# Output stage of the first recurrent scan made inside the scan: bonuses during the rounds, norms and gates between the last chain's steps

## What is computed

```python
g = jax.nn.sigmoid(xg) @ g_up
for direction in range(2):
    a = jax.nn.sigmoid(a_gate0[direction] + xa @ a_gate_up[direction])
    ys.append(wkv7_scan(hs(r), hs(decay), hs(k_dir), hs(v), kk, hs(a), reverse=(direction == 1)))
    a_dirs.append(a)
y = ys[0] + ys[1]
mean = jnp.mean(y, axis=-1, keepdims=True)
var = jnp.mean(jnp.square(y - mean), axis=-1, keepdims=True)
yn = ((y - mean) * lax.rsqrt(var + LNX_EPS)).reshape(B, S, RWKV_WIDTH) * lnx_g + lnx_b
k_bonus = hs(k * (1.0 + (0.5 * (a_dirs[0] + a_dirs[1]) - 1.0) * k_a))
bonus = jnp.sum(hs(r) * k_bonus * r_k, axis=-1, keepdims=True) * hs(v)
return (yn + bonus.reshape(B, S, RWKV_WIDTH)) * g
```

## Time and profile before

| | us |
|---|---|
| median of 3 runs | 2873.18 (2870.74 to 2874.13) |
| the profiled execution's own time | 2872.07 |
| its span | 2869.4 |
| the last full round of the scan (n = 7) | 590.0 to 620.6 |
| the last chain, its products and sum | 620.6 to 637.2 |
| output stage, to the first instruction of the next stage | 637.2 to 667.3 |

### The profile page before, as it was taken

One profiled execution on the slowest core, in us unless ns is written; L12 is line 12 of the kernel. 1 busy time (PEld: TensorE's weight loads), 2 busy tenths in 40 slices (PEclk: granted clock), 3 DMA queues, 4 the chain that ended last, 5 costly groups with the idle time before them and its releaser, 6 DMA issues. The chain is left out here.

```text
span 2869.4 us, 45446 instructions
## 1 busy us (share of the span) xinstructions
PE 2383.1 (83%) x17090; PEld 1374.9 (48%) x17090; DVE 1587.3 (55%) x3634; ACT 1000.6 (35%) x2575; POOL 962.6 (34%) x765
## 2 busy tenths in 40 slices
PE   6998979988898777777777777777779989889996
PEld 3544679975664222332223222332248878643333
DVE  6665465644566666767676666766554453430002
ACT  2122633333433333333333333333245232433433
POOL 0000021113136555555555545545530143223331
PEclk9999989999999999999999999999999966889998
DMA  9942100003069999999999999999963220369994
GB/s 373 374 168 85 56 13 4 5 30 123 32 260 420 420 421 418 417 417 415 413 415 413 413 415 413 415 411 413 415 238 104 98 58 2 123 259 356 378 356 175
DMA packets 174634, 770.12 MB, mean 268 GB/s; under 512 B 33728, under 2 KB 51792, under 8 KB 95056
## 3 DMA queue, kind: packets, MB, share of 16 engines
q0 software_dynamic: 87552, 545.34, 46.5%
q1 hardware_dynamic: 68176, 183.94, 17.3%
q10 hardware_dynamic: 18688, 37.95, 3.7%
HBM read 815.37 MB, written 16.78 MB: 290 GB/s over the span
## 5 line engine op out<-in xcount | busy, mean ns | idle before, releaser
L2108 PE MATMUL bank<-weight_slots,diagonals 128*128 128x512 f32 x1024 | 485.2, 617 | 160.5 <-ACT diagonals L2051 160.5
L1990 DVE SCALAR_TENSOR_TENSOR weight_slots<-weight_slots,h_rows 128x1024 f32<-128x1024 f32 x320 | 392.1, 1225 | 247.8 <-DMA weight_slots<-in_uv,expert_idx 247.0
L1758 POOL DMA_INDIRECT weight_slots<-in_uv,expert_idx x320 | 405.5, 1267 | 353.1 <-PE bank L2108 273.1
L2108 PE MATMUL bank<-expert_rows,first_scores 128*128 128x512 f32 x768 | 370.5, 619 | 147.4 <-ACT first_scores L2051 143.5
L2108 PEld LDWEIGHTS bank<-weight_slots,diagonals 128*128 128x128 f32 x1024 | 188.2, 194 | 449.4 <-ACT diagonals L2051 260.0
L1758 POOL DMA_INDIRECT expert_rows<-in_uv,expert_idx x192 | 283.6, 1477 | 314.2 <-PE bank L2108 185.3
L2040 ACT ACTIVATE expert_act<-expert_dot 128x2 f32<-128x2 f32 x256 | 52.0, 203 | 846.6 <-DVE weight_slots L1990 613.2
L1990 DVE SCALAR_TENSOR_TENSOR expert_rows<-expert_rows,h_rows 128x1024 f32<-128x1024 f32 x192 | 235.3, 1226 | 154.0 <-DMA expert_rows<-in_uv,expert_idx 153.8
L2108 PEld LDWEIGHTS bank<-expert_rows,first_scores 128*128 128x128 f32 x768 | 137.9, 192 | 371.8 <-ACT first_scores L2051 236.7
L682 PE MATMUL bank<-rhs_hi,w_lo 128*128 128x512 f32 (+1 forms) x440 | 178.1, 405 | 33.2 <-POOL rhs_lo L638 18.0
L602 DVE TENSOR_TENSOR w_lo<-weight_slots,w_hi 128x384 fp32r<-128x384 f32 (+3 forms) x152 | 102.7, 682 | 168.7 <-ACT w_hi L547 168.3
(11 more groups left out here) (531 smaller groups left out, 4094.7 us busy)
## 6 DMA issues: line engine op xcount, KB each, us to landing
expert_w<-in_experts SPq DMA_DIRECT2D x55, 1024.0 KB, 12.1
expert_w_more<-in_experts SPq DMA_DIRECT2D x41, 1024.0 KB
mod_w<-in_ada_w ACTq DMA_DIRECT2D x17, 2048.0 KB, 11.8
mod_w<-in_ada_w SPq DMA_DIRECT2D x7, 2048.0 KB, 16.1
weight_slots<-in_w_in SPq DMA_DIRECT2D x6, 2048.0 KB, 17.7
weight_slots<-in_w_in SPq DMA_DIRECT2D x8, 1536.0 KB, 6.7
att_bias<-in_att_bias SPq DMA_DIRECT2D x8, 1024.0 KB, 6.9
weight_slots<-in_w_out SPq DMA_DIRECT2D x4, 2048.0 KB, 8.8
```

Of the source, the lines that this page charges most:

```text
L1758: pool.indirect_dma_start(self.rows[n % self.SLOTS], None, self.core.dram["uv"], bass.IndirectOffsetOnAxis(self.idx[:, t, column:column + ...
L1990: dve.scalar_tensor_tensor(out=u, in0=u, scalar=1.0, in1=hN[:, t, :], op0=ALU.mult, op1=ALU.mult, accum_out=dot[:, j:j + 1]).then_inc(dott ...
L2108: mm = pe.matmul(bank[2 * (t % 2) + half][:, :], diag[j], rows[j][:, D + half * S:D + half * S + S], start=column == 0, stop=column == HK - 1)
```

## The change

`stage_rwkv_output` is removed, and its steps are put into the scan's programs. The bonus of pair f is made by POOL and ACT in the rounds: POOL adds the two rates behind `reads(2f + 1)`, ACT scales the sum behind level 3 of round 2f (`scale_bonus`), and POOL multiplies twice more. The gate's sigmoid is made as exp on ACT in round 3, and 1 + x and a reciprocal on DVE at the end of round 4 (`squash_gate`). In the last chain PE makes a list `SIDE` of 14 matmuls of 128x512, one behind each half-step, with `y_of_chunk` behind each second one, and ACT moves their results. The inverse root is now Sqrt on ACT and a reciprocal on DVE (`invert`), three of which stand between the half-steps of the last chain and the fourth behind it. The third multiply of the bonus goes from DVE to POOL, and the gate is copied out of PSUM by ACT. Results lie in tiles that the scan no longer reads (`a`, `sig`, `kk`). The scan's tiles are placed anew so that the three lent slots are free once the last `end_products` is made, and their loads are issued there; `g_up` is loaded in the rounds.

The diff, cut to its core:

```diff
@@ stage_rwkv
         stage_rwkv_scan(core, zr, sig, a, kk, sel, restart, mixed)
-        stage_rwkv_output(core, zr, a, sel, mixed)
@@ stage_rwkv_scan: placement, order
-        place = [work[:, i, :] for i in range(21)] + [lent[:, i, :] for i in range(8 * RING)]
...
+        ahat, y0, u_sb, states, gain = own[14:19]
+        m_rb, m_rk = [lent[0], own[19]], [lent[1], own[20]]
+        e1, e2, inv, invT, ka, xs = lent[2:8]
...
+        bonus, rstd, gate = [[of[:, f, :] for f in range(PAIRS)] for of in (a, sig, kk)]
+        SIDE = (("centre", 0), ("centre", 1), ("bonus", 0), ("bonus", 1), ("centre", 2), ("sum", 0), ("sum", 1), ("bonus", 2), ("sum", 2),
+                ("gate", 0), ("bonus", 3), ("gate", 1), ("gate", 2), ("gate", 3))
@@ sync
+                sp.wait_ge(summed, 7 + 4)
+                sp.dma_start(g_up, core.dram["g_up"]).then_inc(g_loaded, 16)
+                sp.wait_ge(end_full, 3 * ROUNDS)
+                core.ring.load(sp, core.ring.issued + RING)
@@ vector
+                def squash_gate():
+                    dve.wait_ge(gate_raised, 1)
+                    dve.tensor_scalar(gate_in, gate_in, 1.0, None, ALU.add).then_inc(gate_plus, 1)
+                    dve.wait_ge(gate_plus, 1)
+                    dve.reciprocal(gate_in, gate_in).then_inc(gate_squashed, 1)
+                def invert(f):
+                    dve.wait_ge(rooted, f + 1)
+                    dve.reciprocal(rstd[f], rstd[f]).then_inc(inverted, 1)
...
+                        if n == 0 and l == 1:
+                            columns_of_output()
                     add_y(n - 1)
                     gains(n)
+                    if n == 4:
+                        squash_gate()
+                last = PAIRS - 1
                 for hs in range(14):
                     chain(ROUNDS - 1, hs)
+                    if hs in (8, 9, 11):
+                        invert((8, 9, 11).index(hs))
+                    if hs in (10, 12, 13):
+                        norm((10, 12, 13).index(hs))
                 add_y(ROUNDS - 1)
+                for f in range(last):
+                    add_bonus(f)
+                for f in range(last):
+                    store(f)
+                invert(last)
+                norm(last)
+                add_bonus(last)
+                store(last)
@@ gpsimd
+                def bonus_of(f):
+                    pool.wait_ge(summed, 7 * (2 * f + 1) + 6)
+                    pool.tensor_tensor(bonus[f], a[:, f, :], a[:, f + 4, :], ALU.add).then_inc(rated, 1)
+                    pool.wait_ge(bonus_scaled, f + 1)
+                    pool.tensor_tensor(bonus[f], bonus[f], zr[:, K + f, :], ALU.mult).then_inc(keyed, 1)
+                    pool.wait_ge(keyed, f + 1)
+                    pool.tensor_tensor(bonus[f], bonus[f], zr[:, R + f, :], ALU.mult).then_inc(weighed, 1)
                 for n in range(1, ROUNDS):
                     rates(n)
                     reads(n)
+                    if rev_of(n):
+                        bonus_of(pair_of(n))
+                for f in range(PAIRS):
+                    pool.wait_ge(b_copied, f + 1)
+                    pool.tensor_tensor(bonus[f], bonus[f], zr[:, V + f, :], ALU.mult).then_inc(bonused, 1)
@@ scalar
+                def scale_bonus(f):
+                    if f == 0:
+                        act.wait_ge(cols_made, 2)
+                    act.wait_ge(rated, f + 1)
+                    act.activation(bonus[f], bonus[f], ACT.Identity, scale=cols[:, f, 0:1], bias=cols[:, f, 1:2]).then_inc(bonus_scaled, 1)
...
+                        if l == 3 and not rev_of(n):
+                            scale_bonus(pair_of(n))
+                        if l == 3 and n == 3:
+                            act.wait_ge(summed, 7 * 3 + 4)
+                            act.activation(gate_in, zr[:, 13, :], ACT.Exp, scale=-1.0).then_inc(gate_raised, 1)
...
+                act.activation(core.root[:, 0:1], core.ones[:, 0:1], ACT.Sqrt)
+                for what, f in SIDE:
...
+                square(PAIRS - 1)
+                take_root(PAIRS - 1, S3_BANK)
@@ tensor
                 for hs in range(14):
-                    chain(ROUNDS - 1, hs)
-                y_products(ROUNDS - 1, range(NC))
+                    chain(n, hs)
+                    if hs % 2 == 0:
...
+                        y_of_chunk(n, hs // 2)
+                    side(hs)
+                pe.wait_ge(u_out, 7 * n + 7)
+                y_of_chunk(n, NC - 1).then_inc(y_full, 1)
+                pe.wait_ge(y_added, PAIRS)
+                pe.matmul(C_BANK[last][:, :], centre[:, :], mixed[:, 4 + last, :], start=True, stop=True).then_inc(y_centred, 1)
+                sum_squares(last, S3_BANK)
```

More of the change, by code:

```diff
@@ L1154, in stage_rwkv_scan @@
         z_bank, w_bank = bank[0:2], bank[2:4]
+        C_BANK, S3_BANK = (bank[2], bank[3], bank[1], bank[4]), bank[5]
+        SIDE = (("centre", 0), ("centre", 1), ("bonus", 0), ("bonus", 1), ("centre", 2), ("sum", 0), ("sum", 1), ("bonus", 2), ("sum", 2),
+                ("gate", 0), ("bonus", 3), ("gate", 1), ("gate", 2), ("gate", 3))
+        TURNS = [step for step in SIDE if step[0] != "centre"]
+        side_bank = lambda step: bank[0] if TURNS.index(step) % 2 == 0 else bank[7]
         def columns(ap, m, half):
@@ L1353, in copy_y, with square, take_root @@
                         act.activation(mixed[:, 4 + pair_of(n), :], Y_BANK[:, :], ACT.Copy).then_inc(y_copied, 1)
+                def scale_bonus(f):
[3 more added lines that the diff above has]
+                    act.activation(bonus[f], bonus[f], ACT.Identity, scale=cols[:, f, 0:1], bias=cols[:, f, 1:2]).then_inc(bonus_scaled, 1)
+                def square(f):
+                    act.wait_ge(y_centred, f + 1)
+                    act.activation(rstd[f], C_BANK[f][:, :], ACT.Square).then_inc(squared, 1)
+                def take_root(f, ps):
+                    act.wait_ge(sq_summed, f + 1)
+                    act.activation(rstd[f], ps[:, :], ACT.Sqrt, scale=1.0 / HD, bias=64e-5).then_inc(rooted, 1)
                 decays(0, 0)
@@ L1380, in _ @@
                         act.activation(to, bank[END_BANK[j]][:, :], ACT.Copy).then_inc(end_out, 1)
-                copy_y(ROUNDS - 1)
+                act.activation(core.root[:, 0:1], core.ones[:, 0:1], ACT.Sqrt)
+                for what, f in SIDE:
+                    if what == "centre":
+                        square(f)
+                    elif what == "sum":
+                        take_root(f, side_bank((what, f)))
+                    elif what == "bonus":
+                        act.wait_ge(b_summed, f + 1)
+                        act.activation(bonus[f], side_bank((what, f))[:, :], ACT.Copy).then_inc(b_copied, 1)
+                    else:
+                        act.wait_ge(g_full, f + 1)
+                        act.activation(gate[f], side_bank((what, f))[:, :], ACT.Copy).then_inc(g_copied, 1)
+                square(PAIRS - 1)
+                take_root(PAIRS - 1, S3_BANK)
             @block.tensor
@@ L1490, in chain, with y_of_chunk @@
                         mm.then_inc(u_full, 1)
+                def y_of_chunk(n, k):
+                    c = order(n)[k]
+                    for h in range(2):
+                        pe.matmul(chunk(Y_BANK, c, h), chunk(u_sb if k else y0, c, h), chunk(m_rb[n % 2], c, h), start=True, stop=False)
+                    for h in range(2):
+                        mm = pe.matmul(chunk(Y_BANK, c, h), chunk(vN[n % 2], c, h), chunk(m_rk[n % 2], c, h), start=False, stop=k == 0)
+                    if k >= 1:
+                        for h in range(2):
+                            mm = pe.matmul(chunk(Y_BANK, c, h), chunk(states, k, h), chunk(rho[n % 2], c, h), start=False, stop=True)
+                    return mm
                 def y_products(n, ks):
@@ L1499, in y_products @@
                     for k in ks:
-                        c = order(n)[k]
-                        for h in range(2):
-                            pe.matmul(chunk(Y_BANK, c, h), chunk(u_sb if k else y0, c, h), chunk(m_rb[n % 2], c, h), start=True, stop=False)
-                        for h in range(2):
-                            mm = pe.matmul(chunk(Y_BANK, c, h), chunk(vN[n % 2], c, h), chunk(m_rk[n % 2], c, h), start=False, stop=k == 0)
-                        if k >= 1:
-                            for h in range(2):
-                                mm = pe.matmul(chunk(Y_BANK, c, h), chunk(states, k, h), chunk(rho[n % 2], c, h), start=False, stop=True)
+                        mm = y_of_chunk(n, k)
                     if NC - 1 in ks:
@@ new lines, in sum_squares, with side @@
+                def sum_squares(f, ps):
+                    pe.wait_ge(squared, f + 1)
+                    pe.matmul(ps[:, :], core.headones[:, :], rstd[f], start=True, stop=True).then_inc(sq_summed, 1)
+                def side(i):
+                    what, f = SIDE[i]
+                    if what == "centre":
+                        if f == 0:
```

(21 more changed lines are left out.)

164 lines of the change are left out of this document (38 added, 126 removed).

## The result

| | before | after |
|---|---|---|
| median of 20 runs | 2871.53 us (2867.69 to 2876.40) | 2878.31 us (2874.68 to 2883.06) |
| profiled execution: own time, span | 2872.07, 2869.4 | 2881.73, 2879.9 |

A forecast was written before the change was run, and what follows sets the result against it. PE's queue was taken to bound the rounds, with hand-overs in the last chain and output stage; 9.6 + 3.1 + 8 - 9.9 = +10.8 us on 2872.07 gave 2882.9, so 2884 as median, range 2875 to 2891.

The forecast's parts named there:

- ACT's wait in rounds 2, 4 and 6: Behind level 3, ACT waits for POOL's sum before evacuating level 4, delaying PE's end products: 3.2 us each, 9.6 us.
- The reciprocal at the end of round 4: 1 + x and a 3.33 us reciprocal on DVE precede the chain's first half-step; PE goes on 3.1 us later.
- The clock: Each of four stalls idles PE over 3 us and lowers its clock: 2 us each, 8 us in all.
- round 0: First round of the scan: POOL's sum is early and ACT's 0.8 us lie before level 4, so no cost.
- The tail: From the last chain to the end of the last store: ends 9.9 us earlier, 11.6 at full clock throughout.
- Its first step: Last chain's half-step pairs: a 128x512 matmul holds PE 0.86 us, a pair takes 2.3, half-step 8 starts at 629.8.
- the basis: Forecast's starting time: one execution's own time, 2872.07 us, with the median of the runs taken as 1.1 above it.
- that the clock holds: Rival: PE's clock stays high through the stalls, +2.8 us, 2876, no change that counts; chance 0.16.
- PE catches up the stalls: Rival in the rounds: other waits shorten, PE's queue absorbs the stalls, only the tail counts, 2863 us; chance 0.05.
- the cheap reciprocal: Rival: wide reciprocals take 0.69 us in round 4 and the tail, giving -6 us, 2867; chance 0.04.
- POOL blocks DVE: POOL passes hold up DVE steps in the rounds: none counted; dearer rival +4 us, 2888 to 2890 with its clock alternative, chance 0.16.

The follow-up runs named there:

- the three profiles: The changed kernel, unedited, profiled once for the result and twice more as follow-up; medians 2878.3 and 2880.2 us, ratios 1.0020 and 1.0016 to the kernel before.
- one experiment: Changed kernel with ACT's scaling of the bonus moved behind the evacuation of the xs products in rounds 2f+1; 2897.3 us, ratio 1.0074 to the kernel before.
- the multiplies late: Changed kernel with ACT's scaling behind the xs evacuation and POOL's two bonus multiplies behind `reads` of the next round; 2865.4 us, ratio 0.9965.

## Why the prediction was right in kind and off in size

- **ACT's wait in rounds 2, 4 and 6**: right. 3.48 us of waiting less the 0.38 of before is 3.1 in each of three rounds, 9.3 where 9.6 was summed.
- **The reciprocal at the end of round 4**: 4.50 - 1.77 = 2.7 us, where 3.1 was summed; 1 + x took 0.42 us where 0.6 was taken. Its length, 3.35 where 3.33 was drawn from two widths, was right. From the repeat count of 8 that the Trainium skill states (VectorE: DVE Perf Modes, "First, the fixed hardware budget") the prediction had worked out an estimate of 4.3 us; the trace does not agree, at 3.35.
- **The clock**: rounds 2, 4 and 6 together are 19.8, 18.3 and 19.6 us too long in the three profiles; less the 12.0 us of waits that leaves 7.8, 6.3 and 7.6 for the clock, where 2 us for each of four stalls, 8, was taken. The total was near, the split was not: behind ACT's three stalls the clock was low in every profile, behind the reciprocal only in the first. What the step left out is round 0, which was costed at nothing: in two of the three profiles the low stretch of the earlier trace rows is gone from it, 1.6 us less. The same program shows both lengths there, so this is luck as far as the runs show. So the rounds add up to 18.3 us in all three, of which 6.3 are the clock's. The mean of 2 us a stall hides how wide the price is: behind a shorter gap in PE's work the low level lasted 27 us in one experiment.
- **The tail**: 9.9 was summed, 10.5 is usual and 7.4 in the profile of the changed kernel. Its first step was wrong: "four records take 1.88 us" holds for matmuls of one shape in a row, and a matmul between small ones holds PE for 1.06, not 0.86, which is 0.4 us a pair. The other 0.3 is the chain: its four records between two such matmuls hold PE for 0.26 (626.22 to 626.48 above), where 0.12 was taken for each four, and with a chunk of y 0.61 (627.54 to the next matmul of 128x512 at 628.15), where 0.47 was taken. A pair takes 2.98 us, not 2.3, and half-step 8 came 11.8 us behind the chain's start instead of 9.2. Behind it the clock was better than assumed in most profiles (0.86 and 0.79 in the second), and the two errors cancelled by luck.
- **The size**: 2884 against 2878.3 is 5.7 us. The median of 20 runs before lay 0.5 us under its profiled execution, and not 1.1 over it as that of three did: 1.6 us. The rounds gave 18.3 and not 20.7: 2.4. The tail gave 0.6 more. The remaining 1.1 us are unexplained. Of the rounds' 2.4 us, 0.7 are the waits and 1.7 the clock. So the step that failed is the clock's term: 8 us was summed, 2 for each stall and nothing for round 0, and 6.3 was measured. Next to it stands the basis, one execution and a median of three, with 1.6 us. The forecast itself, +10.8, was a difference of two sums of 20.7 and 9.9, so that small errors in either weigh much in it. The part behind the last store alone took 2198.7 to 2204.0 us in the profiles of this study, in stages that the change does not touch (span less the end of the last store).
- **The rivals**: that the clock holds was wrong for ACT's three stalls (0.50 behind each), and right in two of three profiles for the reciprocal. That PE catches up the stalls is out, with 18.3 us more in the rounds, and so is the cheap reciprocal, at 3.35 us. That POOL blocks DVE cost nothing in the changed kernel, as forecast, but only by where the multiplies fall; in the place where they met DVE's chain steps, the rounds took 247.9 us instead of the 214.7 with the multiplies late. The Trainium skill (SBUF — State Buffer, "Who interferes with whom") says that a DVE step with two SBUF inputs contends with a GpSimd step that reads SBUF, that the shared port pair is an exclusive lock, and that the order of issue decides who blocks. The steps of 1.05, 1.26 and 1.34 us above agree: they began later than POOL's pass and end with it (the first of them is a copy, which the page counts among those that can contend).

## What to carry to other kernels

When an engine with little to do gets work that another engine's step needs, look at what stands ahead of that work in its queue, not at its load: here one step of POOL put ahead of another that waits turned +6.8 us into -6.5, each against the kernel before on the same chip. Price a stall of PE twice, as the wait and as the clock behind it, and keep a wide range on the second. Before giving POOL a pass, find the DVE steps that PE waits for in that place, since a step of 0.28 us can take 1.3.

## What the hardware showed that was not expected

- The low clock has no fixed length. In round 6 of the changed kernel PE stood idle from 600.4 to 603.85; the clock fell 2.1 us into that and stayed low for 6.8 us (602.5 to 609.3, worked out from the clock of the edge windows). After 1.9 us of idle time, spread over 3 us, it was low for 27 us (426.5 to 453.8) with PE busy for 25.56 of 26. Why is open.
- The same stall of PE does not always bring it down: behind the reciprocal, with PE idle for 2.3 to 2.6 us, the clock was low for 3.4 us in the first profile (544.5 to 547.9) and stayed at 1.00 in the second and third.
- The same program, with the same work in round 0, takes 27.7 or 29.2 us there: the clock falls near 403 or it does not.
- A 128x512 matmul between matmuls of 64x64 costs PE 0.2 us more than one in a row of its kind (1.06 and 0.86).
